# The high part of background projection weights, made by ACT at the eviction instead of by POOL

## The reference

```python
    for l in range(DEPTH):
        h = rmsnorm(x, norm_g[l])
        proj = jnp.einsum('bsd,de->bse', h, w_in[l])
        (a_q, a_k, a_v, a_z, b_q, b_k, b_v, b_z,
         c_qkv, c_z, c_b, c_a, gate_logits) = jnp.split(proj, offsets, axis=-1)
...
        y_a = jnp.einsum('bse,ed->bsd', o_a * jax.nn.silu(a_z), w_bo_a[l])
...
        y_b = jnp.einsum('bse,ed->bsd', o_b * jax.nn.silu(b_z), w_bo_b[l])
...
        y_c = jnp.einsum('bse,ed->bsd', o_c * jax.nn.silu(c_z), w_bo_c[l])
...
        merged = gates[:, :, 0] * y_a + gates[:, :, 1] * y_b + gates[:, :, 2] * y_c
        x = x + jnp.einsum('bsd,de->bse', merged, w_out[l])
    return rmsnorm(x, final_g)
```

## Time and profile before

| | us |
|---|---|
| median of 3 runs | 3548.35 |
| lowest, highest | 3545.24, 3555.44 |
| the profiled execution | 3547.25 |
| its span (first to last instruction) | 3545.5 |
| its mean granted TensorE clock | 0.911 of 2.4 GHz |

### The profile page before, as it was taken

One profiled execution on the slowest core, in us unless ns is written; L12 is line 12 of the kernel. 1 busy time (PEld: TensorE's weight loads), 2 busy tenths in 40 slices (PEclk: granted clock), 3 DMA queues, 4 the chain that ended last, 5 costly groups with the idle time before them and its releaser, 6 DMA issues. The chain is left out here.

```text
span 3545.5 us, 42842 instructions
## 1 busy us (share of the span) xinstructions
PE 2922.8 (82%) x15946; PEld 2396.1 (68%) x15946; DVE 1801.0 (51%) x2187; ACT 1134.7 (32%) x1867; POOL 1169.3 (33%) x500
## 2 busy tenths in 40 slices
PE   3979797889859986779978888789887798697896
PEld 2858685667747776757756777667665576585675
DVE  6126464555657652347331555565554683533653
ACT  2113232455534512331011222245543443133211
POOL 2332222222335541036344313223231564202451
PEclk9989897999989998989989999889998899898997
DMA  4232322222235435554322323222223344455442
GB/s 138 78 101 78 90 70 85 83 74 62 83 107 172 138 110 156 144 192 142 113 76 90 101 67 93 85 66 89 69 73 107 125 161 133 126 148 177 143 131 106
DMA packets 403196, 388.30 MB, mean 110 GB/s; under 512 B 91232, under 2 KB 341728, under 8 KB 403040
## 3 DMA queue, kind: packets, MB, share of 16 engines
q1 hardware_dynamic: 364832, 300.26, 29.1%
q10 hardware_dynamic: 38208, 85.99, 6.3%
HBM read 253.99 MB, written 132.19 MB: 109 GB/s over the span
## 5 line engine op out<-in xcount | busy, mean ns | idle before, releaser
L200 PE MATMUL pair<-h_hi,w_hi 128*128 128x512 f32 x1792 | 761.8, 425 | 196.5 <-POOL w_lo L186 84.3
L200 PE MATMUL pair<-h_lo,w_hi 128*128 128x512 f32 x1792 | 729.6, 407 | 0.0
L200 PE MATMUL pair<-h_hi,w_lo 128*128 128x512 f32 x1792 | 725.8, 405 | 0.0
L200 PEld LDWEIGHTS pair<-h_hi,w_hi 128*128 128x128 f32 x1792 | 357.8, 200 | 316.8 <-SPq L130 83.4
L184 POOL TENSOR_TENSOR w_hi<-w_stage,masks 128x1024 fp32r<-128x1024 f32 x108 | 288.2, 2669 | 731.2 <-PE pair L200 541.8
L200 PEld LDWEIGHTS pair<-h_lo,w_hi 128*128 128x128 f32 x1792 | 357.7, 200 | 77.0 <-issue 6.4
L200 PEld LDWEIGHTS pair<-h_hi,w_lo 128*128 128x128 f32 x1792 | 355.3, 198 | 79.8
L186 POOL TENSOR_TENSOR w_lo<-w_stage,w_hi 128x1024 fp32r<-128x1024 f32 x108 | 281.6, 2607 | 8.5
L215 ACT ACTIVATE ev<-pair 128x512 f32<-128x512 f32 x224 | 132.1, 591 | 459.7 <-PE pair L200 459.7
L153 PE MATMUL pair<-h_hi,w_hi 128*128 128x512 f32 x576 | 183.1, 400 | 43.8 <-DVE h_lo L537 29.7
L1093 ACT ACTIVATE diff_p<-pair,diff_stat 128x1024 f32<-128x1024 f32 x128 | 142.8, 1116 | 206.7 <-DVE diff_stat L1166 203.6
(11 more groups left out here) (281 smaller groups left out, 5759.9 us busy)
## 6 DMA issues: line engine op xcount, KB each, us to landing
w_stage<-in_w_in SPq DMA_DIRECT2D x132, 512.0 KB, 5.1
proj<-ev ACTq DMA_DIRECT2D x132, 512.0 KB, 2.6
gate<-proj SPq DMA_DIRECT2D x48, 512.0 KB, 3.5
prep_x<-proj SPq DMA_DIRECT2D x24, 512.0 KB, 3.5
diff_vx<-proj SPq DMA_DIRECT2D x18, 512.0 KB, 4.6
diff_xr<-proj SPq DMA_DIRECT2D x72, 128.0 KB, 3.9
prep_g<-gc_rows SPq DMA_DIRECT2D x16, 512.0 KB, 3.8
qd_t<-prep_eg SPq DMA_DIRECT2D x16, 512.0 KB, 2.6
```

The source lines that it names most:

```text
L200: last = nc.tensor.matmul(bank(self.banks[half]), a[s][:, c, :], b[:, c, w], start=(c == 0 and n == 0), stop=(c == KC - 1 and n == 2))
```

## The change

`Side.split` is taken apart. Its two waits and the making of `w_hi` become `Side.high`, on ACT, as an activation (Copy) from `w_stage` to `w_hi`. `out` calls it behind the DMA of unit k, for unit k + 2 of the turn, or for unit 0 or 1 of the next turn; `more=False`, in the delta rule, leaves the latter out, since no turn follows. `Side.low`, on POOL, waits for `w_hi` alone and makes `w_lo`; it stands where `split` stood in POOL's program. The loads, PE's part and the evictions keep their places.

```diff
@@ -164,8 +164,8 @@
 
             SEMS = ["side_in0", "side_in1", "side_hi", "side_lo", "side_sum", "side_out", "side_put0", "side_put1"]
 
-            def __init__(self, l, q, per, banks=(7, 7)):
-                self.q, self.per, self.banks = q, per, banks
+            def __init__(self, l, q, per, banks=(7, 7), more=True):
+                self.q, self.per, self.banks, self.more = q, per, banks, more
 
                 self.in_slot = [(per + 1 - s) // 2 for s in range(2)]
                 self.w = w_in.rearrange("l (k p) e -> l p k e", p=P)[ds(l, 1)].rearrange("o p k e -> (o p) k e")
@@ -175,13 +175,16 @@
                 sp.wait_ge(self.q["side_lo"], START + turn * self.per + (k - 1 if ahead else max(k - 1, 0)))
                 sp.dma_start(w_stage[k % 2][:], self.w[:, :, ds(column, P)]).then_inc(self.q[f"side_in{k % 2}"], 16)
 
-            def split(self, pool, turn, k, ahead=False):
+            def high(self, act, turn, k, ahead=False):
                 q, s = self.q, k % 2
 
-                pool.wait_ge(q["side_sum"], START + turn * (2 * self.per) + (2 * k - 2 if ahead else max(2 * k - 2, 0)))
-                pool.wait_ge(q[f"side_in{s}"], START + turn * (16 * self.in_slot[s]) + (16 * (k // 2) + 16))
-
-                nc.gpsimd.tensor_tensor(w_hi[s][:], w_stage[s][:], bcast(ones, KC), ALU.mult).then_inc(q["side_hi"], 1)
+                act.wait_ge(q["side_sum"], START + turn * (2 * self.per) + (2 * k - 2 if ahead else max(2 * k - 2, 0)))
+                act.wait_ge(q[f"side_in{s}"], START + turn * (16 * self.in_slot[s]) + (16 * (k // 2) + 16))
+                nc.scalar.activation(w_hi[s][:], w_stage[s][:], ACT.Copy).then_inc(q["side_hi"], 1)
+
+            def low(self, pool, turn, k):
+                q, s = self.q, k % 2
+
                 pool.wait_ge(q["side_hi"], START + turn * self.per + (k + 1))
                 nc.gpsimd.tensor_tensor(w_lo[s][:], w_stage[s][:], w_hi[s][:].bitcast(F32), ALU.subtract)\
                     .then_inc(q["side_lo"], 1)
@@ -218,6 +221,10 @@
                     act.wait_ge(q["side_out"], START + turn * (2 * self.per) + (2 * k + 2))
                     act.dma_start(proj[ds(unit, 1)].rearrange("o p s -> (o p) s"), ev[s][:])\
                         .then_inc(q[f"side_put{s}"], 16)
+                    if k + 2 < self.per:
+                        self.high(act, turn, k + 2)
+                    elif self.more:
+                        self.high(act, turn + 1, k + 2 - self.per, ahead=True)
 
             def finish(self, act, turns):
                 for s in range(2):
@@ -684,9 +691,9 @@
                                 pool.wait_ge(q["x_in"], START + 96 * (3 * g + k + 1))
                                 nc.gpsimd.tensor_tensor(XR[:], XR[:], sin[:], ALU.mult).then_inc(q["sined"], 1)
                             if 2 <= k < 8:
-                                side.split(pool, g, k)
+                                side.low(pool, g, k)
                             if k >= 8:
-                                side.split(pool, g + 1, k - 8, ahead=True)
+                                side.low(pool, g + 1, k - 8)
 
                 @block.tensor
                 def _(pe):
@@ -989,13 +996,13 @@
                         sine(0, n, XR0[n])
                     with pool.Fori(0, 4) as h:
                         for n in range(2):
-                            side.split(pool, h, 2 + n)
+                            side.low(pool, h, 2 + n)
                             sine(h + 1, n)
-                        side.split(pool, h + 1, 0, ahead=True)
+                        side.low(pool, h + 1, 0)
                         pool.wait_ge(q["normed"], START + h + 1)
                         pool.wait_ge(q["stored"], START + 16 * h)
                         nc.gpsimd.tensor_tensor(OUT[:], O[:], ZT[:], ALU.mult).then_inc(q["gated"], 1)
-                        side.split(pool, h + 1, 1, ahead=True)
+                        side.low(pool, h + 1, 1)
 
                 @block.tensor
                 def _(pe):
@@ -1291,10 +1298,7 @@
                 @block.gpsimd
                 def _(pool):
                     def split(k):
-                        if k < PREPARED:
-                            side.split(pool, 0, k)
-                        else:
-                            side.split(pool, 1, k - PREPARED, ahead=True)
+                        side.low(pool, k // PREPARED, k % PREPARED)
 
                     def mask(h, d):
                         pool.wait_ge(q["eg"], START + 2 * h + d + 1)
@@ -1515,7 +1519,7 @@
                 RAW = nc.alloc_sbuf_tensor_at("delta_raw", [P, 32, 32], F32, offset=over)
                 TMP = sb("delta_tmp", [P, 2 * 240])
                 VD = R
-                side = Side(l, q, N_GATE - PREPARED, (6, 7))
+                side = Side(l, q, N_GATE - PREPARED, (6, 7), more=False)
                 units = CONV_UNITS[PREPARED:]
                 tile_of = lambda c, d: c if d == 0 else NT - 1 - c
                 rows32 = lambda b: slice(32 * b, 32 * b + 32)
@@ -1614,7 +1618,7 @@
                         last = nc.gpsimd.memset(X0[d][:], 0.0)
                     last.then_inc(q["zeroed"], 1)
                     for k in range(2, N_GATE - PREPARED):
-                        side.split(pool, 0, k)
+                        side.low(pool, 0, k)
                     for s in range(2):
                         stage, hi, lo = (w[s][:, 0:4, :] for w in (w_stage, w_hi, w_lo))
                         pool.wait_ge(q[f"next_in{s}"], START + 16)
```

## The result

| | before | after |
|---|---|---|
| median, us | 3548.35 | 3577.76 |
| lowest, highest | 3545.24, 3555.44 | 3574.61, 3590.69 |
| the profiled execution's span | 3545.5 | 3576.0 |
| mean granted TensorE clock | 0.911 | 0.902 |

The ratio of after to before is 1.009, with a 95% interval from 1.0067 to 1.0114: the changed kernel is slower by 24 to 40 us.

The account below looks back on a forecast made before the run. TensorE, busy 81 to 87% in every stage, was taken as the bound, so microseconds count where PE waits or slows. +41 − 35 + 12 + 8 = +26 on 3547.25 gave 3573, stated as median 3574; range 3560 to 3590.

Parts of the forecast that it names:

- Full attention, +41: Eight heads: ACT's copy at t=2 costs 1.06, load wait plus copy at t=5 4.1, so 5.1 us a head.
- Prepare, −35: Two prepare layers: fewer POOL instructions beside DVE's convolution taps and earlier low parts gain 17.7 us a layer.
- each POOL instruction that DVE meets costs 2.0: Prepare's convolution taps on DVE: each POOL instruction running beside them lengthens them by 2.0 us.
- The small bound, −13: Prepare's bound for the smaller gain: one meeting a head instead of three, −13 us.
- Delta, +12: Two delta layers: solve 8.5 us shorter, but ACT waiting for unit 6's load delays `moves(0, 0)`; 6.0 us lost a layer.
- Window, +8: Four window-attention turns: copies ahead of `p_hi` at t=1, 6 and 14, less relief at the start; +2.0 us a turn.
- The relief at the start (−1.4 a turn): Window turn's start: POOL's high part of 2.4 goes, ACT's copy ahead of `v_hi` costs 1.05, so 1.4 us gained.
- The terms at t=1 and t=6: Window copies ahead of `p_hi`: 1.45 us a turn at t=1, half of wait plus copy; 0.95 at t=6.
- The stalls hide: Rival, all stages: ACT's waits fall into idle time, only relief is left, −58 us, 3489; chance 0.08.
- Relief and stall cancel: Rival: loads land some 3 us earlier, full attention costs +17 instead of +41, total 3550; chance 0.14.
- Slower than the sum: Rival: longer PE gaps lower its granted clock, 0.90 to 0.88 in full attention, +16 us, 3590; chance 0.12.
- The change doesn't free DVE: Rival, prepare and delta: low parts slide into the high parts' slots, DVE meets as many POOL instructions; about 3635; chance 0.06.

Follow-up runs that it names:

- window_only: The change in window attention alone, other stages split on POOL as in the kernel before: 3572.49 us, ratio 1.0068.
- full_load: As full_only, but SP issues the load of the next head's unit 0 right behind that of unit 3: 3556.32 us, ratio 1.0035 to the kernel before.
- full_only: The change in full attention alone, other stages split on POOL as in the kernel before: 3577.68 us, ratio 1.0092.
- full_load_late: As full_load, but for t>0 ACT's copy stands behind `a_hi` instead of ahead of it: 3543.9 us, ratio 0.9995 to the kernel before.

## Why the prediction was right

Forecast +26 us over the profiled execution and 3574 in the median, measured 3577.76. The sign came from two terms that don't touch each other: what ACT's place in the order costs and what POOL's absence gives. That the total came so near is in part luck: in the profiled execution full attention is 9 us under its term, window attention 9 over, and 5 us stand in merge, where nothing changed and none were forecast.

- *Full attention, +41.* The steady heads lengthen by 5.1 us on average (from the first head's t=0 to the fourth's, 102.7 a head before, 107.8 after), which is the forecast's 5.1. At t=2 it was 1.0; at t=5 the wait was 2.9 to 3.5 after the put, with the copy 4.0 up to the end of the head (22.4 to 26.4 in the first). The stages came to +32, not +41. The prediction left out that the last unit's high and low part on POOL ended the stage: 2.3 us of it went. Its start, up to the first put, was 1.4 us shorter as well (41.8 us in layer 0, before 43.2). The runs show the mechanism: without the wait 20 of 33 us are gone, without the copy's place the rest.
- *Prepare, −35.* Measured −37 in the two stages of after and −38 alone. The step "each POOL instruction that DVE meets costs 2.0" held to the row: 13.26 to 11.25 and 11.31 to 7.28. The period of a steady head was forecast at 53.6 and is 53.4, bound by PE as it said. The extra instruction on POOL put DVE's meetings back, and most of the gain went. The small bound, −13, does not follow from the terms: one meeting a head instead of three gives −1.9, with −6.4 and −1.5 some −10 a layer, −20 in both. Neither the sum nor the range rests on it.
- *Delta, +12.* Measured +14 in after, +16 alone. The solve became 8.6 us shorter in layer 0 (DVE's memset at its end comes 68.9 us after POOL's first instruction of the stage before, 60.4 after), 8.5 forecast. Counted from there the load came 10.4 us earlier, not 8.5, and `moves(0, 0)` 10.5 later, not 12.4; the first chunk was 4.9 late, 5.9 forecast. What is over that in layer 0 is in the last chunks: the step to the seventh took 16.7 us at a clock of 0.90, before 14.1 at 1.00. In layer 1 it is the other way round, 14.0 at 1.00 after and 15.6 at 0.89 before, so that is no work of the change.
- *Window, +8.* The weakest term: +17 in after, +24 alone. Two steps failed. The relief at the start (−1.4 a turn) did not come, because behind the low part the next wait was nearly as late: ACT's eviction, which stands in order behind `q_hi`, released PE at 255.29 instead of 255.09. And the copy for unit 2, which I priced there, holds `v_hi` and through it the whole rotary chain of DMA, POOL and DVE, about 1 us a turn. The terms at t=1 and t=6 were right (1.2 and 1.0 a turn). At t=14 no trace can say: the step over the end of the turn is 37.4 to 39.5 us in traces whose window stage is that of before, 38.4 in window_only and 40.8 in after. With 1 us there and 1 at the start a turn loses 3.8 to 4.2, four of them 15 to 17, at the lower end of the interval of window_only (16 to 33). What makes up the rest stays open.
- *Rivals.* "The stalls hide" falls with PE's own start, 4.0 us later, and with full_load. "Relief and stall cancel" falls, since the load did not come earlier by itself (ACT's copy began 4.6 us after the eviction of t=5, POOL's high part 4.0 before); it is the version that one gets by moving it. "Slower than the sum" is half right: the granted clock of full attention did go from 0.90 to 0.88 and PE's busy time there from 361.7 to 374.3 us, but a steady head grew by no more than the 5.1 forecast: part of the slower work fell where PE had waited at the end of the head (6.29 became 3.99). "The change doesn't free DVE" falls with the taps.

That a busy share says little of this is plain from full_only and full_load_late: the same instructions on ACT, at other places, 3578 and 3544 us. The Trainium skill's advice to look for the engine of highest occupancy first ("Perfetto Trace Analysis", section "Identifying the Most-Contended Engine") puts no price on work that moves between two engines of low occupancy. The gaps between instructions, which the section after it says to trace to their semaphores, are where the cost lay.

## What to carry to other kernels

When work moved from one idle engine to another in this kernel, the price was not its duration but what it waited for and what stood behind it in that engine's order: put the wait's data ahead (the load earlier in its queue) and the work into a gap that ends in another engine's wait. The gain is to be looked for on the engine that shares something with the one relieved, here DVE, whose instructions grew shorter one by one. And after a wait is shortened, ask what is the next to be late: at the start of the window turn the low part ended some 2.4 us earlier, and PE started at 255.29 instead of 255.09, since ACT's eviction came last.

## What the runs showed of the hardware

DVE's taps, with two SBUF inputs, take 1.3 us for 128x1024 and about 2.0 more when they meet an instruction of POOL. Instructions with one of their inputs in PSUM (L1452 in after, 1.22 us; L1448 of before, 1.21 beside POOL) don't change. The Trainium skill has this as an exclusive lock on the shared port pair ("SBUF — State Buffer", section "Who interferes with whom"), and here are its prices. A first tap, with one input of this size (L1468), takes 0.74 alone and 2.90 beside POOL. ACT's copy took 1.06 us in all 108 cases, beside whatever ran (mean 1060 ns on the page, as alone), which agrees with its line that ACT waits on no one.

Unexpected was how much PE lost after pauses of one or two microseconds. The 24 matmuls L1009 at t=2 took 3.12 us before, after a pause of 0.58. Here are windows over such groups of 24 matmuls in the first head of after, where the pauses before them were 1.59 and 2.37 and the groups took 4.62 and 5.44 (the clock is the third figure from the end):

```profile
623.50:628.20 4.70, 4.67 (x26) 4.68 (x27) 2.89 (x6) 3.06 (x5) 0.15 (x1) 0.64 0.00 0
663.70:669.20 5.50, 5.45 (x26) 5.45 (x27) 4.97 (x6) 1.60 (x3) 0.00 (x0) 0.52 0.00 0
```

The same two in the kernel before, with pauses of 0.58 and 0.22:

```profile
617.20:620.40 3.20, 3.20 (x27) 3.20 (x28) 2.48 (x4) 1.82 (x3) 2.25 (x1) 1.00 0.00 0
652.50:655.70 3.20, 3.13 (x26) 3.14 (x27) 3.17 (x4) 0.00 (x0) 0.00 (x0) 1.00 0.00 0
```

And the second in full_load, with a pause of 0.27:

```profile
654.20:657.50 3.30, 3.22 (x27) 3.22 (x28) 3.27 (x4) 0.00 (x0) 0.00 (x0) 1.00 0.00 0
```

The granted clock there was 1.00 before, that is the level of 2.4 GHz, and 0.64 and 0.52 after, mostly the level of 1.2 GHz. In the 6.9 us ahead of the first pause it had been 1.00 in after as well. In full_load, where the copy of t=2 still stands ahead of `a_hi`, the pause there is 1.58 and the clock again 0.64. In full attention much of that was hidden, since PE waits for DVE at the end of the head anyway (6.29 fell to 3.99). In window attention such stretches come in kernels with and without the change, as shown above, so what the change adds to them there is not shown.
